# A two-block transformer on one core: weight units, token sums and roots where a stage begins with a normalisation

## The reference

```
layer 0:  x += rms(MLA attention(rms(x))) ; x += rms(swiglu(rms(x)))
          shared k, v = rms(x) @ w_kv
layer 1:  x += rms(chunked attention(rms(x), k, v)) ; x += rms(swiglu(rms(x)))
block 2:  h = rms(x); attention over three branches, and a convolution of 31 taps
          x += (g_a * y_attn + g_b * y_conv) @ w_out
          x += (silu(a) * v) @ w_down, (a, v) = causal 3-tap conv(rms(x) @ w_up)
out = rms(x)
rms(z) = z / sqrt(mean over the 1024 features of z*z + 1e-6) * gain
```

## Time and profile before

| | |
|---|---|
| median of 3 runs | 2223.71 us |
| the profiled execution | 2222.8 us, its span 2220.7 us |
| TensorE busy | 2088.1 us, 94% of the span |
| VectorE, ScalarE, GpSimd busy | 1041.0, 745.0, 751.8 us |
| mean granted TensorE clock | 0.965 of full speed |
| share of the chain that ended last | TensorE 80%, VectorE 14%, ScalarE 3% |

### The profile page before, as it was taken

The page is one execution under the profiler, slowest core; times in us unless marked ns, Lnnn a source line. Parts: engine busy times, 40 slices in busy tenths (PEclk is TensorE's granted clock), DMA queues, the critical chain, the costliest instruction groups (busy, mean ns, idle before and its releaser), DMA issues.

```text
span 2220.7 us, 22496 instructions
## 1 busy us (share of the span) xinstructions
PE 2088.1 (94%) x8948; PEld 1599.9 (72%) x8948; DVE 1041.0 (47%) x1620; ACT 745.0 (34%) x1197; POOL 751.8 (34%) x311
## 2 busy tenths in 40 slices
PE   6898999999988998999999989879899999999998
PEld 4554778888866776678888867657555687888886
DVE  5543254442126554354442138992444447777511
ACT  4444332222224444332222232212545334333321
POOL 2211334444432332334444423431101243444442
PEclk9998999999999999999999999988799999999999
DMA  3410222223221221222332223221000122233322
GB/s 131 133 58 29 76 67 95 95 98 102 95 76 58 94 89 64 76 76 95 103 97 95 95 67 114 67 67 38 29 20 29 39 95 86 95 95 97 102 95 85
DMA packets 51815, 178.59 MB, mean 80 GB/s; under 512 B 5472, under 2 KB 5488, under 8 KB 51456
## 3 DMA queue, kind: packets, MB, share of 16 engines
q1 hardware_dynamic: 45264, 163.07, 22.8%
q10 hardware_dynamic: 6448, 14.09, 1.9%
HBM read 175.00 MB, written 6.33 MB: 82 GB/s over the span
## 4 chain that ended last, share of the span: by engine, by line
PE 80%; DVE 14%; ACT 3%; issue 1%; DMA 0%; POOL 0%; ACTq 0%; DVEq 0%; SPq 0%
PE bank L352 22%; PE bank L353 22%; PE bank L354 22%; DVE tmp L1394 5%; PE bank L375 4%; PE bank L440 2%; PE bank L426 2%; PE bank L466 1%; DVE hl L483 1%; DVE x L928 1%; DVE tmp L1698 1%; DVE tmp L926 1%; PE bank L1083 1%; PE bank L1097 1%; DVE rs L479 1%
## 5 line engine op out<-in xcount | busy, mean ns | idle before, releaser
L341 POOL TENSOR_TENSOR wlo<-raw,whi 128x1024 fp32r<-128x1024 f32 x307 | 751.6, 2449 | 1447.2 <-ACT whi L336 1447.2
L352 PE MATMUL bank<-hh,whi 128*128 128x512 f32 x1576 | 636.9, 404 | 56.5 <-DVE hl L483 30.2
L336 ACT ACTIVATE whi<-raw 128x1024 fp32r<-128x1024 f32 x307 | 325.3, 1060 | 1001.6 <-PE bank L354 991.0
L353 PE MATMUL bank<-hl,whi 128*128 128x512 f32 x1576 | 622.2, 395 | 0.0
L354 PE MATMUL bank<-hh,wlo 128*128 128x512 f32 x1576 | 621.6, 394 | 0.0
L352 PEld LDWEIGHTS bank<-hh,whi 128*128 128x128 f32 x1576 | 301.1, 191 | 160.9 <-issue 52.6
L353 PEld LDWEIGHTS bank<-hl,whi 128*128 128x128 f32 x1576 | 301.0, 191 | 64.6 <-issue 4.6
L354 PEld LDWEIGHTS bank<-hh,wlo 128*128 128x128 f32 x1576 | 301.0, 191 | 64.7
L460 DVE TENSOR_TENSOR tmp<-bank,rs 128x512 f32<-128x512 f32 x159 | 109.3, 690 | 227.7 <-PE bank L354 223.1
L352 PE MATMUL bank<-fh,whi 128*128 128x512 f32 x528 | 205.4, 389 | 0.0
L353 PE MATMUL bank<-fl,whi 128*128 128x512 f32 x528 | 205.4, 389 | 0.0
(11 more groups left out here) (215 smaller groups left out, 2111.2 us busy)
## 6 DMA issues: line engine op xcount, KB each, us to landing
raw<-stream SPq DMA_DIRECT2D x307, 512.0 KB, 3.3
bias_scratch<-rel_scratch ACTq DMA_DIRECT2D x1, 4096.0 KB, 19.6
biasB<-bias_scratch ACTq DMA_DIRECT2D x16, 256.0 KB, 2.8
x<-x_in SPq DMA_DIRECT2D x2, 1024.0 KB, 10.0
w<-w_in ACTq DMA_DIRECT2D x2, 1024.0 KB, 5.9
out<-y ACTq DMA_DIRECT2D x8, 256.0 KB, 2.2
cst<-consts_in ACTq DMA_DIRECT2D x1, 577.5 KB, 7.3
gn<-gains_in ACTq DMA_DIRECT2D x1, 318.5 KB, 4.6
```

What stands on the lines that cost most here:

```text
L336: e.activation(whi[u % 2][:, :], raw[u % 2][:, :], ACT.Copy).then_inc(*w_hi.done(u))
L341: e.tensor_tensor(wlo[u % 2][:, :], raw[u % 2][:, :], whi[u % 2][:, :].bitcast(F32), ALU.subtract)\
L352: e.matmul(o, wh, h, start=first, stop=False)
L353: e.matmul(o, wh, l, start=False, stop=False)
```

## The change

- `slot` and `own_slot_free`: the first two units of the stages F0, B, F1, C and F2 get `whi`/`wlo` buffers of their own, in space that is free then; the other units alternate in the two old pairs. `round_unit` calls are moved so that four units are prepared before such a stage begins; ScalarE's order at the end of a stage changes for it.
- `join_pe` takes three units: for each tile of x it multiplies three blocks, into three banks. In F0, F1 and F2 the units are gate 0, up 0 and gate 1 (banks 2, 3, 0), in B the values, keys and queries of pair 0, in C the branch gates and the two convolution halves.
- The squares in the pass are summed token-wise (`token_sums_pe`, four matmuls of one moving column). The root is taken of four columns, inverted as four columns, and spread by four matmuls whose stationary operand is one column repeated and whose moving operand is the identity (`spread_tokens_pe`). In F0, F1 and F2 this spreading (`join_root_pe`) stands behind up 1 in TensorE's order, in C behind the first gate tile, in B directly behind the pass. ScalarE copies the bank to `rs[0]`.
- `token_root_pe`: the first filling goes, the others become 128 columns wide (2, 3 and 12 of them), the diagonal on VectorE becomes the same spreading on TensorE.
- In B both pairs of halves are made in the one pass; the pair-0 values are turned after the pair-0 scores.
- The merged branches go to `mh` and `ml` instead of `hh` and `hl`, so that the halves of x for F2 are made tile by tile during `w_out`.

The diff, cut to its core:

```diff
     turn = {}
+    FIRST = {"F0": 26, "B": 92, "F1": 124, "C": 190, "F2": 241}
+    OWN_AT = {"F0": R + 72 * KB, "B": R, "F1": R + 48 * KB, "C": R, "F2": R + 48 * KB}
+    slot, before = [], []
+    last_in = [None, None]
+    for u in range(n_units):
+        own = [n for n in FIRST if u - FIRST[n] in (0, 1)]
+        if own:
+            at = OWN_AT[own[0]] + 8 * KB * (u - FIRST[own[0]])
+            slot.append((sb(f"own_hi{u}", [P, 1024], at, F32R), sb(f"own_lo{u}", [P, 1024], at + 4 * KB, F32R)))
+            before.append(None)
+        else:
+            j = 0 if last_in[0] is None or (last_in[1] is not None and last_in[0] < last_in[1]) else 1
+            slot.append((whi[j], wlo[j]))
+            before.append(last_in[j])
+            last_in[j] = u
...
-        if u >= 2:
-            e.wait_ge(*proj.at(("unit", u - 2)))
-        e.activation(whi[u % 2][:, :], raw[u % 2][:, :], ACT.Copy).then_inc(*w_hi.done(u))
+        if before[u] is not None:
+            e.wait_ge(*proj.at(("unit", before[u])))
+        own_slot_free(e, u)
+        e.activation(slot[u][0][:, :], raw[u % 2][:, :], ACT.Copy).then_inc(*w_hi.done(u))
...
-            e.matmul(bank[5][:, :], ones, cst[:, 0:T], start=True, stop=True)
+            e.matmul(bank[5][:, 0:P], ones, ident, start=True, stop=True)
+    def token_sums_pe(e, bk, src, first, last):
+        for t in range(QT):
+            mm = e.matmul(bank[bk][:, t:t + 1], src[:, t * P:(t + 1) * P], ones[:, 0:1], start=first and t == 0,
+                          stop=last and t == QT - 1, skip_group_check=True)
+        return mm
+    def spread_tokens_pe(e, bk, key, col):
+        e.wait_ge(*stats.at((key, "tokens")))
+        for t in range(QT):
+            mm = e.matmul(bank[bk][:, t * P:(t + 1) * P], stat[:, col + t:col + t + 1].to_broadcast([P, P]), ident,
+                          start=True, stop=True)
+        mm.then_inc(*summed.done((key, "inverse")))
...
-        fill_clock(e, 2)
-        e.wait_ge(*formed.at((key, "diagonal")))
-        e.matmul(bank[7][:, :], ones, tmp[7][:, :], start=True, stop=True).then_inc(*summed.done((key, "inverse")))
-        fill_clock(e, 2)
+        token_sums_pe(e, 7, tmp[(KD - 1) % 2], False, True).then_inc(*summed.done((key, "tokens")))
+        fill_clock(e, 3)
+        spread_tokens_pe(e, 7, key, 12)
+        fill_clock(e, 12)
...
         e.reciprocal(stat[:, 12:16], stat[:, 12:16]).then_inc(*stats.done((key, "tokens")))
...
         for m in range(KD):
-            round_unit(e)
-            e.wait_ge(*evicted.at((key, m)))
+            if m == KD - 2:
+                round_unit(e)
+                round_unit(e)
             if m < KD - 1:
+                round_unit(e)
+                e.wait_ge(*evicted.at((key, m)))
                 square_tile(e, key, m, y[:, m, :])
+        e.wait_ge(*evicted.at((key, KD - 1)))
         token_root_act(e, key, y[:, KD - 1, :])
+        round_unit(e)
...
-    def join_pe(e, key, bk, out_key):
-        u = next_unit(e)
+    def join_pe(e, key, outs, added=False):
+        us = [next_unit(e) for _ in outs]
         for k in range(KD):
-            e.wait_ge(*low.at((key, k)))
-            mm = product(e, u, k, bank[bk][:, :], hh[:, k, :], hl[:, k, :], k == 0, k == KD - 1)
-            if k == KD - 1:
-                mm.then_inc(*proj.done(out_key, ("unit", u)))
-            e.wait_ge(*squared.at((key, k)))
-            pe_sum(e, 6, tmp[k % 2][:, :], k == 0, k == KD - 1, (key, k))
-    def join_act(e, key, gain):
+            for i, (u, (bk, out_key, second)) in enumerate(zip(us, outs)):
+                e.wait_ge(*low.at((key, "second", k) if second else (key, k)))
+                h, l = (h2h, h2l) if second else (hh, hl)
+                mm = product(e, u, k, bank[bk][:, :], h[:, k, :], l[:, k, :], k == 0, k == KD - 1)
+                if k == KD - 1:
+                    mm.then_inc(*proj.done(out_key, ("unit", u)))
+            if not added:
+                e.wait_ge(*squared.at((key, k)))
+                token_sums_pe(e, 6, tmp[k % 2], k == 0, k == KD - 1).then_inc(*summed.done((key, k)))
+        if added:
+            e.wait_ge(*formed.at((key, "sq", KD - 1)))
+            token_sums_pe(e, 6, tmp[7], True, True).then_inc(*summed.done((key, KD - 1)))
+    def join_root_pe(e, key):
+        spread_tokens_pe(e, 6, key, 16)
+    def join_act(e, key, gain, second=None):
         for k in range(KD):
             e.wait_ge(*joined.at((key, k)))
             e.activation(hh[:, k, :], x[:, k, :], ACT.Copy, scale=gg(gain, k)).then_inc(*high.done((key, k)))
             if k >= 2:
                 e.wait_ge(*summed.at((key, k - 2)))
             act_square(e, tmp[k % 2], x[:, k, :], (key, k))
-        act_root(e, rs[0], (key, KD - 1))
+            if second:
+                e.activation(h2h[:, k, :], x[:, k, :], ACT.Copy, scale=gg(second, k)).then_inc(*high.done((key, "second", k)))
+        e.wait_ge(*summed.at((key, KD - 1)))
+        e.activation(stat[:, 16:20], bank[6][:, 0:QT], ACT.Sqrt, scale=1.0 / D, bias=cc("eps"))\
+            .then_inc(*made.done((key, "root")))
+        e.wait_ge(*summed.at((key, "inverse")))
+        e.activation(rs[0][:, :], bank[6][:, :], ACT.Copy).then_inc(*made.done((key, "inv")))
...
-    def join_dve(e, key, before, post, gain):
+    def join_dve(e, key, before, post, gain, second=None):
         e.wait_ge(*summed.at((before, "inverse")))
         join_tile(e, key, post, 0)
         for k in range(KD):
             if k + 1 < KD:
                 join_tile(e, key, post, k + 1)
             dve_low(e, hl[:, k, :], x[:, k, :], gg(gain, k), hh[:, k, :], (key, k))
-        dve_mean(e, rs[0], 6, D, (key, KD - 1))
-        dve_inverse(e, rs[0], (key, KD - 1))
-        e.wait_ge(*stats.at(((key, KD - 1), "inv")))
+            if second:
+                dve_low(e, h2l[:, k, :], x[:, k, :], gg(second, k), h2h[:, k, :], (key, "second", k))
+        join_root_dve(e, key)
+    def join_root_dve(e, key):
+        e.wait_ge(*made.at((key, "root")))
+        e.reciprocal(stat[:, 16:20], stat[:, 16:20]).then_inc(*stats.done((key, "tokens")))
+        e.wait_ge(*made.at((key, "inv")))
     def ffn_pe(e, key, conv):
         for j in range(KF):
             b0 = 2 if j == 0 else 0
+            if j == 0:
+                continue
             if j >= 2:
                 e.wait_ge(*evicted.at((key, "gate", j - 1)))
-            if j:
                 project(e, b0, hh, hl, (key, "gate", j))
-            if j >= 2:
                 e.wait_ge(*evicted.at((key, "up", j - 1)))
             project(e, b0 + 1, hh, hl, (key, "up", j))
+            if j == 1:
+                join_root_pe(e, {"F0": "j0", "F1": "j2", "F2": "x2"}[key])
...
     def ffn_act(e, key, conv):
         for j in range(KF):
-            round_unit(e)
+            if j:
+                round_unit(e)
             if conv:
                 for r, part in enumerate(("gate", "up")):
-                    if r:
+                    if r and j:
                         round_unit(e)
                     e.wait_ge(*evicted.at((key, part, j)))
                     if j:
...
                                  bias=gg("fdwb", r * KF + j)).then_inc(*made.done((key, part, j)))
                 e.wait_ge(*formed.at((key, "gate", j)))
             else:
-                round_unit(e)
+                if j:
+                    round_unit(e)
                 e.wait_ge(*evicted.at((key, "gate", j)))
             g = tmp[4 if conv else 2]
             e.activation(g[:, :], g[:, :], ACT.Silu).then_inc(*made.done((key, "silu", j)))
         for half in range(2):
-            for kk in range(KF // 2):
+            for kk in range(KF // 2 - half):
                 round_unit(e)
+                if half and kk == 8:
+                    round_unit(e)
+                    round_unit(e)
             for m in range(4):
                 mi = 4 * half + m
                 if mi < KD - 1:
...
                     square_tile(e, (key, "down"), mi, (x if conv else y)[:, mi, :])
         e.wait_ge(*evicted.at((key, "down", KD - 1)))
         token_root_act(e, (key, "down"), (x if conv else y)[:, KD - 1, :])
+        round_unit(e)
...
     def b_first_pe(e):
-        join_pe(e, "j1", 5, ("vB", 0))
-        project(e, 0, hh, hl, ("kB", 0))
-        u = next_unit(e)
-        for k in range(KD):
-            e.wait_ge(*low.at(("pre1", k)))
-            mm = product(e, u, k, bank[1][:, :], h2h[:, k, :], h2l[:, k, :], k == 0, k == KD - 1)
-        mm.then_inc(*proj.done(("qB", 0), ("unit", u)))
-        b_values_pe(e, 0)
+        join_pe(e, "j1", ((5, ("vB", 0), False), (0, ("kB", 0), False), (1, ("qB", 0), True)))
+        join_root_pe(e, "j1")
...
     def b_pe(e):
         b_first_pe(e)
         for p in range(PAIRS_B):
             more = p + 1 < PAIRS_B
-            e.wait_ge(*evicted.at(("qB", p)))
+            e.wait_ge(*evicted.at(("qB", p) if p else ("kB", 0)))
             pair_scores_pe(e, ("B", p), qB[p % 2], kB[p % 2])
             if more:
```

(45 more changed lines are left out.)

62 lines of the change are left out of this document (25 added, 37 removed).

## The result

| | median | runs |
|---|---|---|
| before | 2222.34 us (2219.12 to 2227.43) | 4 |
| after | 2246.43 us (2245.53 to 2250.01) | 4 |

The ratio is 1.0109, 95% interval [1.0086, 1.0132]. The forecast was 2240.7 us in a range of 2222 to 2252. The profiled execution after took 2245.53 us, its span is 2243.4 us, its mean granted clock 0.957.

What follows compares the result with a forecast made beforehand. The chain of waits was taken as four fifths TensorE, so only stage borders counted. Stage terms summed to +17.0 us on the profiled 2222.8, giving 2239.8; with the median 0.9 above, 2240.7 us, range 2222 to 2252.

Steps and rivals of the forecast that it cites:

- The pass: Each pass over x: TensorE-bound, tiles 2.95 us apart including 0.91 us of token sums; a pass alone gains 2.8 us.
- The rival of free sums: In the passes, the sums' weight loads hide behind products, tiles take 2.05 us: 2216.3 us in all; chance 0.17.
- The wait of gate 2: In F0, F1 and F2, TensorE waits for scaling of gate 1 to free its bank: 5 to 7, F2 about 11 us.
- F0: Stage up to gate 2: later root, bank wait and 2.0 us of half clock make it +6.1 us (+2.5 to +8.8).
- Root before j0: End of stage ahead of F0's pass: VectorE starts at 272.9, between 271.9 at full clock and 274.0 at half clock.
- the last root: Last normalisation: gains 0.75 us by the same steps as other stage ends, at full clock (-1.5 to +0.3).
- F2: Stage from x2: third unit late, then root, bank wait and half clock put gate 2 at +9.2 us (+4.5 to +10.6).
- B: Stage to pair 1's first product: gains 5.8 and 2.45, less 1 for the clock: -7.3 us (-9.3 to -4.3).
- C: Stage with the taps: first tap tile +4.8 us after VectorE's start, less 2.45 gained: +2.35 us (0 to +4.4).
- VectorE's taps set the end: In C, the stage's end follows VectorE's taps; first tap tile moves from 33.35 to 38.15 us after VectorE's start.
- the short waits: Rival for the stage borders: full clock kept, bank and units at lower bounds, +4 to +10, about 2231 us; chance 0.17.
- the cold passes: Rival: one-column sums and narrow fillings drop the clock during four passes, +4 us each, 2257 us; chance 0.12.

Runs made afterwards that it cites:

- experiment 1: Kernel after the change, with gate 2 and up 2 of the three feed-forwards moved to free banks: 2243.67 us, ratio to before 1.0106.
- experiment 2: Kernel after the change, with gate 2's weight unit rounded by ScalarE before it waits for the root's inverse: 2246.58 us, ratio 1.011.
- experiment 3: Kernel after the change, with both a free bank for gate 2 and its unit rounded ahead of the root: 2226.54 us, ratio 1.0024.
- Experiment 8: Kernel after the change, with the token root's fillings 512 columns wide, in number and place as before the change: 2246.67 us, ratio 1.0134.
- experiment 5: Kernel with free bank and early unit of gate 2, and in F2 alone also the units behind it rounded earlier: 2227.48 us, ratio 1.0036.
- experiment 7: Kernel after the change, with F2's pass over x alone undone, so the root is spread ahead of up 0: 2237.64 us, ratio 1.0099.
- experiment 6: Kernel of experiment 5, with C's root also spread directly behind the pass instead of behind gate 0: 2224.31 us, ratio 1.0028.
- experiment 4: Kernel after the change, with the root's spreading on TensorE moved ahead of up 1 in F0, F1 and F2: 2227.21 us, ratio 1.004.

## Why the prediction was right, and where its sizes were off

- **The pass.** Tiles forecast 2.95 us apart, measured 2.97; a set of sums 0.91, measured 0.95 as a group (2.97 less nine products of 0.227 is 0.93). The rival of free sums falls. The Trainium skill's "TensorE: Matmul & The Clock Gate", section "Step-by-step: what each phase is for", says that the next weights load while a matmul runs. In the middle of a stream of products, too, that did not make the one-column sums free: they cost the 0.93 us.
- **The wait of gate 2.** Right in mechanism and nearly in size: from the copy's end to the free bank 6.5 us, forecast 6.1; the wait 7.17 us, where 13.1 - 6.4 = 6.7 was forecast. Experiments 1 to 3 show what the forecast named side by side: the late unit and the full bank, each enough to hold gate 2. The Trainium skill's "ScalarE: Activation LUTs", section "What ACT_TABLE_LOAD costs", has 1.38 us of drain with each load; here silu starts at 310.07, 0.01 us after the table load's end; no drain of 1.38 us stands behind it, and the measurement decides.
- **F0, +8.8 for +6.1.** Root before j0 10.0 us from the last eviction, forecast 7.9: it ran at half clock. I had put the value between both clocks. That is the mis-sized term: 2.1 of the 2.7 us. Even my bound for half clock, 9.0, was too low: I gave root and reciprocal 0.5 us and left out that the three fillings behind the sums run at half clock too. The reciprocal had ended at 271.34; the spreading waited for them until 272.10:

```profile
269.12 1.71 PE L867 MATMUL bank<-cst,tmp 128*128 128x1 f32 x8
270.68 1.63 PE L862 MATMUL bank<-cst 128*128 128x128 f32 x6
272.10 1.91 PE L875 MATMUL bank<-cst,stat 128*128 128x128 f32 x8
```

  It returns in F1 (8.2 for 7.5) and in the last root (8.0 for 5.3), where -0.75 was forecast and +1.9 came. Experiment 8 brought the first and the last back, not that before j2. Which level of the clock a root gets isn't explained by these runs.
- **F2, +10.8 for +9.2.** The wait came as forecast, 11.75 us at gate 2 for about 11. But I took it for the cause, a bank and a unit that come late, and it isn't: experiments 3 and 5 cure both and leave the stage at +10.0 and +11.3, while experiment 7, with the first scaling moved forward, leaves +1.4. VectorE's scalings of gate 0 and gate 1 stand 10.35 us apart (1876.69 and 1887.04; in F0 5.76, 308.80 and 314.56), TensorE's two projections take 10.88. So the chain of scaling, convolution and silu is about as long for a product as TensorE's work, and a first scaling that comes 9.6 us later can hardly be worked off. In the kernel after TensorE has no gap over 0.3 us behind gate 2 to the end of F2: what is lost ahead of it stays lost.
- **B, -5.8 for -7.3.** The root before j1 gained 2.8 us (2.45 forecast), the pass to pair 1 2.7 (4.8 net of the clock). TensorE waited 2.01 us for the scalings and made the scores at half clock. The chain of waits has (start, us, what), where it was 2.43:

```profile
698.41 4.64 PE bank L1131 x16
```

  I had allowed 1 us for this.
- **C, -0.9 for +2.35.** The first tap tile came 4.7 us later after VectorE's start, as forecast (4.8), and the root before gained 2.7. The step that isn't borne out is "VectorE's taps set the end": 3 us were regained behind the first tap tile. In all seven kernels with this C some was regained, but between 1.5 and 8.5 us, so 3 us is no size to build on. What regains them stays open; that VectorE's start does count, experiment 6 suggests in its profile.
- Of the rivals, the short waits fell with the 7.17 us, the cold passes with a clock of 1.00 in the pass. The short waits could be had: experiments 3 and 4 are that rival, made by hand, at some 2227 where it was priced at 2231.

## What to carry to other kernels

Merging projections into one pass over the input delays the first result that the next engines can take. In F0 and F1 it saved next to nothing even with its wait cured (+1.6 and +0.4, and without the longer roots ahead of them -0.5 and -0.6, the same within 0.1 us in the other four kernels with bank and unit), where I had counted 2.8 us for a pass alone. In B it won 2.7. Before doing it, follow the chain from that first result to the buffer that TensorE asks for next. If the stage behind is as slow on the other engines as on TensorE, the delay stays in full, as in F2. When two things are late, each cure alone measures nearly nothing (3 and 0 us of 20): test both together before dropping either.
